# A two-layer hybrid decoder trunk: attended rows held in SBUF and turned inside the output projection, its weights loaded during attention, the first norm joined to the input projection

## The reference, cut to what matters

```python
xn = rms_norm(h, mix_norm_g[0])
rq, rk, rv, rg, nq_, kc, vc, ks, vs, kw, vw, ng = jnp.split(xn @ w_in, cuts, axis=-1)   # 3352 columns
y_ret = rms_norm(retention(rq, rk, rv), ret_norm_g) * silu(rg)          # 512 columns
y_nsa = native_sparse_attention(nq_, kc, vc, ks, vs, kw, vw, ng, ...)   # 512 columns
h = h + jnp.concatenate([y_ret, y_nsa], axis=-1) @ w_out                # 1024 x 1024
xn = rms_norm(h, ffn_norm_g[0])
h = h + hierarchical_moe(xn, ...)   # top-1 of 4 groups, top-2 of 8 experts
```

## Time and profile before

| | us |
|---|---|
| median of 3 runs | 2274.65 (2274.07 to 2274.82) |
| the profiled execution | 2273.94 |
| its span in the trace | 2272.3 |

### The profile page before, as it was taken

The page is one execution under the profiler, slowest core; times in us unless marked ns, Lnnn a source line. Parts: engine busy times, 40 slices in busy tenths (PEclk is TensorE's granted clock), DMA queues, the critical chain, the costliest instruction groups (busy, mean ns, idle before and its releaser), DMA issues. The chain is left out here.

```text
span 2272.3 us, 26062 instructions
## 1 busy us (share of the span) xinstructions
PE 1887.1 (83%) x9536; PEld 1561.2 (69%) x9536; DVE 1238.0 (54%) x1634; ACT 859.1 (38%) x917; POOL 315.6 (14%) x228
## 2 busy tenths in 40 slices
PE   5999977976689997985999991499999958999970
PEld 5888876766577786764888771388887746888750
DVE  5212215545555443555999883432234547999863
ACT  5001004311233333114888872311111116888850
POOL 0000003000100000112444320000000112443310
PEclk8999996656799998996999995699999978999995
DMA  5321135230000005427999964511124319999937
GB/s 203 124 85 66 51 99 179 69 69 3 1 10 10 10 6 197 167 84 283 371 377 374 366 235 184 188 37 48 53 65 151 126 70 381 387 381 374 365 116 296
DMA packets 147604, 378.36 MB, mean 167 GB/s; under 512 B 40302, under 2 KB 75374, under 8 KB 122766
## 3 DMA queue, kind: packets, MB, share of 16 engines
q1 hardware_dynamic: 118614, 325.02, 38.8%
q0 software_dynamic: 19680, 34.22, 4.0%
q10 hardware_dynamic: 9216, 17.93, 2.1%
HBM read 333.44 MB, written 77.20 MB: 181 GB/s over the span
## 5 line engine op out<-in xcount | busy, mean ns | idle before, releaser
L1049 DVE TENSOR_TENSOR ex_gu_lo<-experts_w_gu,ex_gu_hi 128x2048 fp32r<-128x2048 f32 x96 | 219.7, 2289 | 43.6 <-ACT ex_gu_hi L994 43.2
L940 PE MATMUL ex_ps_h<-ex_gu_hi,ex_x_hi 128*128 128x512 f32 x512 | 215.6, 421 | 30.2 <-DVE ex_x_lo L1053 29.6
L940 PE MATMUL ex_ps_h<-ex_gu_hi,ex_x_lo 128*128 128x512 f32 x512 | 204.2, 399 | 0.0
L940 PE MATMUL ex_ps_h<-ex_gu_lo,ex_x_hi 128*128 128x512 f32 x512 | 203.6, 398 | 0.0
L994 ACT ACTIVATE ex_gu_hi<-experts_w_gu 128x2048 fp32r<-128x2048 f32 x96 | 183.4, 1910 | 24.8 <-PE ex_ps_h L940 18.1
L377 PE MATMUL in_ps<-in_w_lo,in_xT_hi 128*128 128x512 f32 (+1 forms) x448 | 168.3, 376 | 0.0
L377 PE MATMUL in_ps<-in_w_hi,in_xT_hi 128*128 128x512 f32 (+1 forms) x448 | 168.2, 375 | 0.0
L377 PE MATMUL in_ps<-in_w_hi,in_xT_lo 128*128 128x512 f32 (+1 forms) x448 | 168.1, 375 | 0.0
L1217 PE MATMUL conv_ps<-oddx_xT_hi,conv_w_hi 128*128 128x512 f32 x384 | 150.6, 392 | 14.1 <-DVE conv_w_lo L1173 14.1
L360 DVE COPY in_stage<-in_ps 128x512 f32<-128x512 f32 (+1 forms) x56 | 36.8, 657 | 224.3 <-PE in_ps L377 224.3
L1217 PE MATMUL conv_ps<-oddx_xT_lo,conv_w_hi 128*128 128x512 f32 x384 | 150.2, 391 | 0.0
(11 more groups left out here) (305 smaller groups left out, 4135.9 us busy)
## 6 DMA issues: line engine op xcount, KB each, us to landing
experts_w_gu<-in_moe_w_gate SPq DMA_DIRECT2D x48, 1024.0 KB
experts_w_gu<-in_moe_w_up SPq DMA_DIRECT2D x48, 1024.0 KB
experts_w_d<-in_moe_w_down SPq DMA_DIRECT2D x48, 1024.0 KB
in_region<-in_ev_w_in SPq DMA_DIRECT2D x12, 1024.0 KB, 5.3
proj<-in_stage ACTq DMA_DIRECT2D x48, 256.0 KB, 2.0
odd_region<-in_od_w_in SPq DMA_DIRECT2D x24, 512.0 KB, 3.9
stream<-out_h SPq DMA_DIRECT2D x16, 512.0 KB
xn<-out_xn SPq DMA_DIRECT2D x16, 512.0 KB, 2.8
```

The costliest lines, as they stand in the source:

```text
L940: last = pe.matmul(ps_h[:, u % 2, :], a[:, u % 2, k, :], w[:, k, :], start=(k == 0 and j == 0), stop=(k == KT - 1 and j == 2))
L1049: dve.tensor_tensor(lo, raw(u % B), hi.bitcast(F32), ALU.subtract).then_inc(piece_lo[piece], 1)
```

## The change

Four things are changed together.

1. `norm_transpose` and `project` of the input are one stage, `norm_project`. The rows of x are loaded tile by tile between the first two weight pieces. Column block 0 is done tile by tile while the later tiles are normed and turned: after the product of tile t TensorE does the transposes of tile t+2. PSUM holds two tiles for transposes and four banks for products, where products had eight.
2. Attention keeps its rows in `attended`, an SBUF buffer that now outlives it. SP stores nothing there and instead loads all of the output weights (both 512-column blocks, 4 MB) at the start of attention into a region that is now one for the whole program. Retention's gate, query, key and value rows lie in that region before. `mixer` holds only the 512 columns of retention.
3. The stage `tr0` is gone. `project_and_route` of layer 0 gets `rows=(attended, mixer)`: SP loads the eight retention tiles (256 KB each) into `retained`, and TensorE turns tile t+1 with `turn_rows(t+1)` in the middle of tile t. The turned rows share `ps_t` with `turn`. ScalarE makes `x_hi` (`take_rows`), VectorE `x_lo` (`rest_of_rows`), two buffers each.
4. Warm-up matmuls there and in `norm_project` are 24 of 128x128 on the identity. The semaphore clear that stood behind `tr0` is gone with it; the one behind retention clears three ranges and not one.

Layer 1's `out1` goes through the same function with `rows=None` and keeps its order; its second weight block is loaded by `ahead.load(sp, 1)`.

```diff
@@ norm_project, VectorE and TensorE
+                norm(0)
+                norm(1)
+                low(0, 0)
+                rest(0)
+                low(0, 1)
+                for t in range(NT):
+                    if t + 2 < NT:
+                        norm(t + 2)
+                    if t + 1 < NT:
+                        rest(t + 1)
+                    if t in (3, 4):
+                        low(1, t - 3)
+                    if t:
+                        take(0, t - 1)
...
+                warm_up(pe, ps[:, BANKS - 1, 0:P], cst.ident[:], cst.ident[:], 24)
+                turn(0)
+                turn(1)
+                for t in range(NT):
+                    pe.wait_ge(x_low, t + 1)
+                    product(0, t, wide[0], t - BANKS + 1 if t >= BANKS else None, lambda c: c + 1)
+                    if t + 2 < NT:
+                        turn(t + 2)
@@ project_and_route, SP
-                for c in range(2):
-                    at = slice(c * HALF, (c + 1) * HALF)
-                    sp.dma_start(raw[1][:, at, :], w_k[:, at, COLS:2 * COLS]).then_inc(raw_loaded[2 + c], 16)
+                if rows is not None:
+                    for t in range(NT):
+                        sp.dma_start(retained[:, t, :], mixer[t * P:(t + 1) * P, :]).then_inc(retained_loaded[t], 16)
+                else:
+                    ahead.load(sp, 1)
@@ project_and_route, ScalarE
+                def take_rows(t):
+                    act.wait_ge(x_turned, t + 1)
+                    if t >= 2:
+                        act.wait_ge(multiplied, 2 * (t - 2) + 2)
+                    act.activation(x_hi[:, t % 2, :, :], ps_t[:], ACT.Copy).then_inc(x_high, 1)
...
                 for t in range(NT):
                     take_turned(t)
+                    if rows is not None and t + 2 < NT:
+                        take_rows(t + 2)
                     squares(t)
@@ project_and_route, VectorE
+                def rest_of_rows(t):
+                    dve.wait_ge(x_high, t + 1)
+                    dve.tensor_tensor(x_lo[:, t % 2, :, :], ps_t[:], x_hi[:, t % 2, :, :].bitcast(F32), ALU.subtract
+                                      ).then_inc(x_low, 1)
...
                 for t in range(NT):
                     add_residual(t, 0)
+                    if rows is not None and t + 1 < NT:
+                        rest_of_rows(t + 1)
                     if t:
                         choose(t - 1)
                     add_residual(t, 1)
@@ project_and_route, TensorE
+                def turn_rows(t):
+                    pe.wait_ge(retained_loaded[t], 16)
+                    pe.wait_ge(hT_ready, max(0, t - 1))
+                    pe.wait_ge(x_low, t)
+                    for k in range(KT):
+                        here = retained[:, t, k * P:(k + 1) * P] if k < RET_W // P else attended[:, t, k * P - RET_W:(k + 1) * P - RET_W]
+                        last = pe.transpose(ps_t[:, k, :], here, cst.ident[:])
+                    last.then_inc(x_turned, 1)
...
                 def turn(t):
                     pe.wait_ge(h_ready, 2 * t + 2)
                     pe.wait_ge(hT_ready, t)
+                    if rows is not None:
+                        pe.wait_ge(x_low, min(NT, t + 2))
...
                 for t in range(NT):
                     multiply(t, 0, 0)
                     if t:
                         turn(t - 1)
                     multiply(t, 0, 1)
+                    if rows is not None and t + 1 < NT:
+                        turn_rows(t + 1)
...
@@ sparse_attend, SP
-                for t in range(NT):
-                    sp.wait_ge(mixed, 2 * G * (t + 1))
-                    sp.dma_start(y_out[t * P:(t + 1) * P, RET_W:RET_W + NSA_W], keep.o[:, t, :]).then_inc(stored, 16)
-                sp.wait_ge(stored, 16 * NT)
+                for b in range(2):
+                    ahead.load(sp, b)
```

More of the change, by code:

```diff
@@ L329, in _ @@
+                store(0, NT - 1)
+                for b in range(1, n_blocks):
                     if b + 1 < n_blocks:
-                        high(b + 1)
+                        for c in range(2):
+                            high(b + 1, c)
                     for t in range(NT):
-                        act.wait_ge(tile_out[t], b + 1)
-                        act.dma_start(out[t * P:(t + 1) * P, b * COLS:b * COLS + n], stage[:, t % 4, 0:n]
-                                      ).then_inc(stage_stored[t % 4], 16)
+                        store(b, t)
@@ L350, in _ @@
+                take(0, NT - 1)
+                for b in range(1, n_blocks):
                     for t in range(NT):
                         if t == 2 and b + 1 < n_blocks:
[L352 to L359 removed]
@@ L381, in _, with turn @@
-                with pe.Fori(0, full // 2) as i:
-                    for u in range(2):
-                        body(u, i, COLS)
-                for b in range(full // 2 * 2, n_blocks):
-                    body(b % 2, b // 2, wide[b])
+                def turn(t):
+                    pe.wait_ge(normed, t + 1)
+                    if t >= 2:
+                        pe.wait_ge(x_low, t - 1)
+                    for k in range(KT):
+                        last = pe.transpose(ps_t[:, t % 2, k, :], xn[:, t % 2, k * P:(k + 1) * P], cst.ident[:])
+                    last.then_inc(turned, 1)
@@ new lines, in product @@
+                def product(u, t, n, taken, ready):
+                    if taken is not None:
+                        pe.wait_ge(staged, taken)
+                    at = slice(t * P, (t + 1) * P)
+                    for k in range(KT):
+                        if t == 0 and k % HALF == 0:
+                            pe.wait_ge(lo_ready[u], ready(k // HALF))
+                        for j, (a, w_part) in enumerate(((xT_hi, w_hi), (xT_hi, w_lo), (xT_lo, w_hi))):
+                            last = pe.matmul(ps[:, t % BANKS, 0:n], a[:, k, at], w_part[:, u, k, 0:n],
+                                             start=(k == 0 and j == 0), stop=(k == KT - 1 and j == 2))
+                    last.then_inc(multiplied, 1)
@@ L387 @@
+                for b in range((full - 1) // 2 * 2 + 1, n_blocks):
+                    for t in range(NT):
+                        product(b % 2, t, wide[b], b * NT + t - BANKS + 1, lambda c: 2 * (b // 2) + c + 1)
 CAP = S
```

282 lines of the change are left out of this document (177 added, 105 removed).

## The result

| | before | changed |
|---|---|---|
| median, first measurement | 2274.74 us (8 runs) | 2282.86 us (2278.01 to 2286.55, 8 runs) |
| ratio to before | | 1.0029, 95% interval 1.0017 to 1.0041 |
| the profiled execution, its span | 2273.94, 2272.3 | 2278.01, 2276.3 |
| busy TensorE, mean granted clock | 83%, 0.888 | 83%, 0.887 |

The change makes the kernel slower by 0.29%, 6.6 us by the ratio and 8.1 by the medians. Three groups of rows show where that comes from.

What follows compares the result with a forecast made beforehand. Input projection was taken as TensorE-bound, an `out0` pass as bound by a three-engine ring, narrowly. Terms -12.8 - 23.4 + 6.1 + 28.8 + 13.8 = +12.5 on the 2274.65 us median gave 2287 us, range 2270 to 2297.

Steps and rivals of the forecast that it cites:

- Front: Joined norm and input projection: eighth product copied out at 71.6 against 84.37, -12.8 us; bounds -16 to -8.
- near 28: Sign of being right: first product of the input projection copied out near 28 us (28.2).
- Between attention and `out0`: The 21 us stage, the store ahead and the clear behind it go, so `out0` starts at 867.2: -23.4 us.
- Start of `out0`: First residual-row turn 25.5 us into `out0`, before 19.4, waiting on late constants: +6.1 us; bounds +3.4 to +8.
- Six passes: `out0`, tiles 0 to 5: squares wait for the copy of turned rows; 4.8 us more per pass, +28.8 us.
- the lower clock: TensorE's waits in `out0` bring half clock at each pass's start: 2.3 us a pass, +13.8; bounds 0 to 20.
- the ring: Chain over TensorE, ScalarE and VectorE in an `out0` pass, turn to `count`: 11.7 us before, 4.8 us more per pass.
- At nothing: Weight load in attention under 1 us, clear behind retention below 1 us; remaining retention, layer 1 and experts keep their order.
- a sign of being wrong: A change in the length of retention, attention or layer 1 by more than 3 us would show the prediction wrong.
- the clock holds: Rival: the clock stays up through the waits in `out0`; 2273 us, or 2270 with the better front; 12%.
- The ring does not close: Rival: rows of tile t+2 taken before squares of tile t can start, `out0` passes under 15.5 us; 2250 us; 5%.
- The lower clock did not persist: Rival judged: low clock covers both halves of block 0 and more, 4 to 6 us per pass; 2297 to 2310; 6%.

Runs made afterwards that it cites:

- filling the gaps: Kernel turning rows at the start of a tile, plus 11 and 9 identity matmuls in the first stage's gaps; 2248.22 us, ratio 0.9888.
- The filled wait: Changed kernel plus 16 identity matmuls on TensorE ahead of the wait at `count` in tiles 1 to 6 of `out0`; 2273.02 us, ratio 0.9990.
- The two kernels with another order: Changed kernel with ScalarE's squares ahead of the copy of turned rows, 2250.28 us; changed kernel with rows turned at the start of a tile, 2250.65 us.
- the moved line: Changed kernel with ScalarE's squares of tile t put ahead of its copy of the turned rows of tile t+2; 2250.28 us, ratio 0.9885.

## Why the prediction was right, and where it was off

It said 2287 us, 0.78 for slower. Its mechanism stands: the front and the gap gain about 36 us, and the start and the passes of `out0` lose more. Term by term:

- **Front**, -12.8: measured -13.2 in the first trace (84.37 to 71.13). The second tile was squared at 12.83 (13.4 predicted), the first product started at 19.6 (20.3), the eighth copy stands at 71.13 (71.6). The sign it gave for the first copy, "near 28", was wrong: it came at 30.77, because VectorE's order puts the row remainder of tile 2 ahead of it. That cost nothing, since TensorE did not wait for the bank. The lower clock in it was put at 2.5 us; filling the gaps gave back 1.6.
- **Between attention and `out0`**, -23.4: measured -23.8.
- **Start of `out0`**, +6.1: measured +5.8, but by another path. The constants landed 18.3 us into the stage, not 20.5, and held nothing: from the first product to the first turn TensorE did not stop. What made the turn late is that the first product came 9.0 us into the stage, behind 5.6 us of warm-up and the turn, the copy and the remainder of tile 0, and that it ran into 3.4 us at the lower clock. The step as written ("SP now issues eight retention loads ahead") is wrong; the size was luck.
- **Six passes**, +28.8, and **the lower clock**, +13.8: together 42.6, measured from the first to the seventh turn 131.15 - 90.17 = 41.0 (879.12 to 1010.27, and 910.02 to 1000.19). The filled wait separates them: 19.6 - 14.8 = 4.8 us a pass for the ring, as worked out, and 21.64 - 19.58 = 2.1 for the clock, where 2.3 was taken. The two kernels with another order show the parts of the 4.8: 3.7 and 1.1, predicted as 3.6 and 1.2.
- **At nothing**: this is the step that failed, twice and in opposite directions. The stages from retention to attention were put at under 1 us and cost about 2 by the two traces, 4 or more by the others. Everything behind `out0` was put at no change and is 5.5 us shorter, of it about 2 in the first experts' stage (347.9 and 347.6 us in place of 349.5 and 349.6) and the rest in pieces of 2 or less. Apart from the 1.5 us of clock at the start of attention no run tells why; both stay open. Without them the terms gave +12.5 and the traces +9.5. The two errors partly cancel in the total. The prediction names a change of over 3 us in retention, attention or layer 1 as a sign of being wrong: retention and attention each stay under it, layer 1 does not (883.5 and 881.1 us before, 878.8 and 878.5 changed).

Two statements of the text put on record are not so. The clear does not stand behind retention with three ranges; it moved behind the preparation. And `out0` does not start 23 us sooner and end 25 later, since that leaves out the front: by the prediction's own terms it starts 36 us sooner and ends 12.5 later, and in the traces it started 36.7 sooner (853.92 against 890.61) and the experts' first load came 10.3 later (1049.58 against 1039.25).

Of the rivals, "the clock holds" is excluded by the granted clock of 0.80 to 0.91 in the passes. It would have given 2273, and the filled wait, which makes it true in all passes but the first, has 2273.02. "The ring does not close" would have given 2250; it is what the moved line makes of the kernel, 2250.28. That both agree within 1 us is luck, since stages that the sums put at nothing moved by up to 6 us. The lower clock did not persist over both halves of block 0 in most passes; where it lasted 6.1 us, the pass was 1.2 to 1.6 us longer than its neighbours. Of the Trainium skill (TensorE: Matmul & The Clock Gate, HAM oscillation) the prediction took that a loop whose TensorE waits in every pass pays for the lower clock in each. The section describes waits for a DMA; here TensorE waits for VectorE, and these traces agree, with 2.1 us a pass.

## What to carry to other kernels

When an operation is moved into a loop, look where it lands in the order of each engine, not only of the engine it loads: here a copy of 1 us, put ahead of the squares though its input comes 3.6 us later, held them back and cost 3.7 us a pass. The wait that this made on TensorE cost twice, once as a wait and once in the clock behind it. Spare matmuls in the wait gave the second part back; another order on ScalarE removed 3.7 of the 4.8 us of the first part and all of the second behind the waits of about 1 us.

## What the runs showed that was not expected

- 16 matmuls of 128x128 whose result nothing reads, 3.73 us long, in a wait of about 4.8 us kept the granted clock at 1.00 and shortened a pass by 2.1 us. In the first stage 20 of them lifted the clock from 0.57 to 1.00, and retention started 1.6 us sooner.
- The same wait can be followed by either clock. At the first `count` of `out0` TensorE waited 2.08 us in both traces of the kernel before; the next 3.2 us had a granted clock of 1.00 in one and 0.61 in the other, and from this `count` to the next turn it was 2.88 and 4.46 us.
- A longer warm-up is not free. The 24 matmuls at the start of `out0` took 5.6 us and stood ahead of the first turned rows; with 12 ahead and 8 behind, and the constants issued earlier, the first turn came 4.2 us sooner.
- The same code of retention, preparation and attention took from 537.1 to 543.8 us in the eight traces of changed kernels. A difference of 5 us in a total does not point to the stage that was edited; the stage's own length does.
